# Two transformer blocks on one core: the shared expert's products spread over group two, the last scatter halved, one weight split moved

## The reference, cut to what matters

```python
def hier_moe(h, ...):
    t = h.reshape(-1, d)
    # each token: the best group, then the best 2 of its 8 experts, with weights "combine"
    a = jnp.einsum('nd,edf->nef', t, w_gate)
    b = jnp.einsum('nd,edf->nef', t, w_up)
    hid = jax.nn.silu(a) * b * combine[:, :, None]
    routed = jnp.einsum('nef,efd->nd', hid, w_down)
    shared = (jax.nn.silu(t @ w_sh_gate) * (t @ w_sh_up)) @ w_sh_down
    return (routed + shared).reshape(bsz, slen, d)

# first_block, at its end
h = h + rms_norm(ffn, post_ffn_norm[l])
# second_block, at its start
u = rms_norm_2(h, norm_mix[l])
proj = u @ w_in[l]
z_pool, q, k, v, g_pool, g_attn = jnp.split(proj, splits, axis=-1)
```

## Time and profile before

| what | us |
| --- | --- |
| median of 3 runs | 738.94 (738.7 to 742.1) |
| the profiled execution | 737.79 |
| its span in the profile | 736.0 |
| TensorE busy in the span | 667.2 (91%) |
| VectorE, ScalarE, POOL busy | 331.8, 280.9, 46.9 |
| weight stream | 182.23 MB in all, mean 248 GB/s over the span |

### The profile page before, as it was taken

The page is one execution under the profiler, slowest core; times in us unless marked ns, Lnnn a source line. Parts: engine busy times, 40 slices in busy tenths (PEclk is TensorE's granted clock), DMA queues, the critical chain, the costliest instruction groups (busy, mean ns, idle before and its releaser), DMA issues.

```text
span 736.0 us, 10953 instructions
## 1 busy us (share of the span) xinstructions
PE 667.2 (91%) x4473; PEld 517.5 (70%) x4473; DVE 331.8 (45%) x607; ACT 280.9 (38%) x529; POOL 46.9 (6%) x68
## 2 busy tenths in 40 slices
PE   8999899898677895778889999999989999999996
PEld 5979787734212741133359999989789999999994
DVE  8676555631101011011056566647755544445554
ACT  7655563312001010011055666573555433344432
POOL 1000102000001000000037200000000000000000
PEclk9999999999777999688999999999999999999998
DMA  9926309599999959999995444335525455455201
GB/s 355 419 92 228 115 8 420 231 364 415 423 420 421 403 217 422 423 420 420 423 420 205 172 145 143 115 123 197 196 104 183 172 183 211 179 174 192 93 1 58
DMA packets 26145, 182.23 MB, mean 248 GB/s; under 512 B 3040, under 2 KB 3168, under 8 KB 4464
## 3 DMA queue, kind: packets, MB, share of 16 engines
q1 hardware_dynamic: 25344, 178.81, 62.1%
q10 hardware_dynamic: 752, 2.73, 0.9%
HBM read 180.48 MB, written 1.05 MB: 247 GB/s over the span
## 4 chain that ended last, share of the span: by engine, by line
PE 66%; DMA 19%; DVE 7%; ACT 4%; issue 2%; POOL 1%; SPq 0%; DVEq 0%; POOLq 0%; ACTq 0%
PE ps L1377 64%; DMA ring<-stream_dram 18%; PE ps L1380 2%; DVE ring_r L362 2%; ACT single L355 1%; DMA vec<-small_dram 1%; DVE work L1331 1%; ACT work L768 1%; DVE work L1334 0%; DVE turned L1290 0%; POOL stat L810 0%; DVE turned L1350 0%; POOL stat L872 0%; ACT work L696 0%; ACT turned L773 0%
## 5 line engine op out<-in xcount | busy, mean ns | idle before, releaser
L1377 PE MATMUL ps<-turned,single 128*128 128x256 f32 (+1 forms) x1312 | 240.1, 285 | 2.9 <-DVE turned L1350 1.2
L1377 PEld LDWEIGHTS ps<-turned,single 128*128 128x128 f32 x1312 | 203.0, 189 | 6.0 <-issue 2.9
L1377 PE MATMUL ps<-turned,ring_r 128*128 128x256 f32 (+1 forms) x656 | 185.5, 283 | 0.0
L362 DVE TENSOR_TENSOR ring_r<-ring,single 128x1024 fp32r<-128x1024 f32 x134 | 160.8, 1243 | 49.4 <-ACT single L355 49.4
L1377 PE MATMUL ps<-ring,work 128*32 128x512 f32 (+2 forms) x814 | 134.1, 666 | 32.9 <-DMA ring<-stream_dram 28.5
L355 ACT ACTIVATE single<-ring 128x1024 fp32r<-128x1024 f32 x134 | 133.8, 1049 | 2.2 <-DMA ring<-stream_dram 1.7
L1377 PEld LDWEIGHTS ps<-turned,ring_r 128*128 128x128 f32 x656 | 124.0, 189 | 0.0
L1377 PEld LDWEIGHTS ps<-ring,work 128*32 128x32 f32 (+1 forms) x814 | 38.1, 127 | 107.9 <-DMA ring<-stream_dram 62.5
L1377 PE MATMUL ps<-single 128*128 128x512 f32 (+1 forms) x299 | 64.6, 363 | 3.6 <-DVE single L1244 2.0
L1377 PEld LDWEIGHTS ps<-single 128*128 128x128 f32 x299 | 47.0, 197 | 28.8 <-issue 15.6
L1377 PE MATMUL ps<-single,turned 128*128 128x512 f32 (+3 forms) x208 | 59.8, 365 | 3.1 <-DVE turned L1054 1.8
(11 more groups left out here) (227 smaller groups left out, 576.3 us busy)
## 6 DMA issues: line engine op xcount, KB each, us to landing
ring<-stream_dram SPq DMA_DIRECT2D x161, 1024.0 KB, 11.8
work<-stream_dram SPq DMA_DIRECT2D x5, 1024.0 KB, 13.0
turned_w<-stream_dram SPq DMA_DIRECT2D x2, 1024.0 KB, 13.6
gain<-gains_dram ACTq DMA_DIRECT2D x3, 512.0 KB, 8.2
cst<-consts_dram ACTq DMA_DIRECT2D x1, 1066.0 KB, 9.0
h<-x_dram SPq DMA_DIRECT2D x2, 512.0 KB, 4.1
out_dram<-work SPq DMA_DIRECT2D x4, 256.0 KB, 2.0
vec<-small_dram SPq DMA_DIRECT2D x1, 451.5 KB, 5.8
```

The source lines that it names most:

```text
L362: dve.tensor_tensor(ring_r[:, place, a], ring[:, place, a], w_hi[k % HIGHS][:, a].bitcast(F32), ALU.subtract).then_inc(s["wlo_done"], 1)
L1377: return pe.matmul(o, lhsT, rhs, start=start, stop=stop, **kw)
```

## The change

It has three parts.

1. The shared gate entry comes behind the third gate/up entry of group 1's second half, the up entry behind the sixth, the shared down entry behind the group's last. The products of each stand at the same places on TensorE, in banks 6 and 7; SiLU and the hidden product stand ahead of the half's own; TensorE waits for them ahead of `down`. The turning (now into bank 4) and the shared down products stay between groups 1 and 2. POOL's four memsets wait for an earlier count of `used`.
2. In the last half of the last group, `scatter(p, 0)` stands between the third and the fourth down entry, in place of the 4 idle products there. The squares and the gain products of column half 0 stand ahead of the copy and the split of column half 1. `used` for the last entry is counted by the other half of the scatter.
3. VectorE splits the first half of entry `SPLIT1` behind the last low part of u, ahead of the second. TensorE does all products with that entry's high weights first (two chunks), then those with its low weights.

```diff
-SHARED_GROUP = 2
-SHARED_AT = MOE_AT + SHARED_GROUP * MOE_GROUP
+SHARED_GROUP = 1
+SHARED_BEHIND = {2: 0, 5: 1}
+SH_GATE_AT = MOE_AT + SHARED_GROUP * MOE_GROUP + Q_SLOTS + 3
+SH_UP_AT = SH_GATE_AT + 4
+SH_DOWN_AT = MOE_AT + (SHARED_GROUP + 1) * MOE_GROUP + 2
...
+            def sum_squares(n):
+                for i in range(NT):
+                    act.wait_ge(s["moe_done"], 1 + n * (i + 1))
+                    act.activation(xn2[:, i, column_half(n)], ps[:, 2 * i + n, :], ACT.Square, accum_out=(ssc, ssc2)[n][:, i:i + 1]
+                                   ).then_inc(s["ss_done"], 1)
...
                 for p in range(PAIRS):
+                    if shared and p == PAIRS - 1:
+                        shared_silu()
                     act.wait_ge(s["gu_ps"], it * PAIRS + (p + 1))
...
                     for n in range(2):
+                        if ending and p == PAIRS - 1 and n:
+                            sum_squares(0)
                         act.wait_ge(s["y_ps"], it * (2 * PAIRS) + (2 * p + n + 1))
...
-            pool.wait_ge(used, SHARED_AT)
+            pool.wait_ge(used, ASIDE_END)
...
+            def with_moe_gain(i, n):
+
+                dve.wait_ge(s["ss_done"], 6 + 2 * n + i)
+                a = column_half(n)
+                dve.tensor_tensor(mixb[:, i, a], ps[:, 2 * i + n, :], gain[:, a], ALU.mult).then_inc(s["gmoe_done"], 1)
...
                 for p in range(PAIRS):
+                    if shared and p == PAIRS - 1:
+                        shared_hidden()
                     dve.wait_ge(s["sg_done"], it * PAIRS + (p + 1))
...
                     for n in range(2):
+                        if ending and p == PAIRS - 1 and n:
+                            with_moe_gain(0, 0)
+                            with_moe_gain(1, 0)
                         dve.wait_ge(s["yh_done"], it * (2 * PAIRS) + (2 * p + n + 1))
...
-            for i, n in ((0, 0), (0, 1), (1, 0), (1, 1)):
-
-                dve.wait_ge(s["ss_done"], (6, 8, 7, 9)[2 * i + n])
...
+            with_moe_gain(0, 1)
+            with_moe_gain(1, 1)
             for i in range(NT):
                 dve.wait_ge(s["rs_done"], 5 + i + 1)
-                dve.wait_ge(s["gmoe_done"], 2 * i + 2)
+                dve.wait_ge(s["gmoe_done"], 3 + i)
...
-            split_low_half(dve, SPLIT1, 0)
             dve.wait_ge(s["rs_done"], 7 + 1)
...
-            split_low_half(dve, SPLIT1, 1)
-            for n in range(1, 8):
+            for n in range(0, 8):
                 split_low(dve, SPLIT1 + n)
...
+            def shared_gate_up(b):
+
+                n = (SH_GATE_AT, SH_UP_AT)[b]
+                slot_ready(pe, n)
+                for i in range(NT):
+                    for t in range(DT):
+                        last = mm(ps[:, 6 + i, b * FF:(b + 1) * FF], tT[:, t, i * P:(i + 1) * P],
+                                  home(n)[:, t * FF:(t + 1) * FF], t == 0, t == DT - 1)
+                        if i == t == 0:
+                            last.then_inc(used, 1)
+                    if b:
+                        last.then_inc(s["sgu_ps"], 1)
...
                         if t == 1 and p:
                             scatter(p - 1, 1)
+                        if shared and p and t in SHARED_BEHIND:
+                            shared_gate_up(SHARED_BEHIND[t])
...
                     for n in range(2):
                         for j in range(FF // P):
-                            keep_warm(p)
+                            if not (n and j):
+                                keep_warm(p)
...
+                            if split_scatter(p) and n and j == 0:
+                                scatter(p, 0)
...
-                            if n == i == k == 0:
+                            if i == k == 0 and n == int(split_scatter(p)):
                                 end.then_inc(freed, 1)
...
+                    if shared and p:
+                        pe.wait_ge(s["hs_done"], NT)
                     down(p)
-                    scatter(p, 0)
+                    if not split_scatter(p):
+                        scatter(p, 0)
...
-            for c in range(4):
-                chunk(ps[:, c, 0:TOK], SPLIT1 + c // 2, c % 2, (u_hi, u_lo), frees=1 if c == 2 else 0,
-                      turned_from=11 if c == 0 else None).then_inc(s["z2_ps"], 1)
+            for c in range(2):
+
+                pe.wait_ge(s["whi_done"], 2 * SPLIT1 + c + 1)
+                for t in range(DT):
+                    if c == 0:
+                        pe.wait_ge(s["turn_dve"], 11 + t + 1)
+                    w = w_hi[SPLIT1 % HIGHS][:, c * D + t * P:c * D + (t + 1) * P]
+                    mm(ps[:, c, 0:TOK], w, u_hi[:, t, :], t == 0, False, skip_group_check=True)
+                    mm(ps[:, c, 0:TOK], w, u_lo[:, t, :], False, False, skip_group_check=True)
+            for c in range(2):
+                split_ready(SPLIT1, c)
+                for t in range(DT):
+                    last = mm(ps[:, c, 0:TOK], split_pair(SPLIT1)[1][:, c * D + t * P:c * D + (t + 1) * P], u_hi[:, t, :],
+                              False, t == DT - 1, skip_group_check=True)
+                last.then_inc(s["z2_ps"], 1)
+            for c in range(2, 4):
+                chunk(ps[:, c, 0:TOK], SPLIT1 + 1, c % 2, (u_hi, u_lo), frees=1 if c == 2 else 0).then_inc(s["z2_ps"], 1)
```

More of the change, by code:

```diff
@@ L373, in entry_at @@
         def entry_at(n):
-            if n < MOE_AT or n >= SHARED_AT + 3:
+            if n < MOE_AT or n > SH_DOWN_AT:
                 return n
-            return n + 3 if n < SHARED_AT else SH_GATE + n - SHARED_AT
+            shared = {SH_GATE_AT: SH_GATE, SH_UP_AT: SH_UP, SH_DOWN_AT: SH_DOWN}
+            return shared[n] if n in shared else n + 3 - sum(at < n for at in shared)
         def place2(n):
@@ L658, in shared_silu, with column_half, moe_group @@
                     act.wait_ge(s["sgu_ps"], i + 1)
-                    act.activation(sg_s[:, i, :], ps[:, 4 + i, 0:FF], ACT.Silu, scale=rsb[:, i:i + 1]
+                    act.activation(sg_s[:, i, :], ps[:, 6 + i, 0:FF], ACT.Silu, scale=rsb[:, i:i + 1]
                                    ).then_inc(s["ssg_done"], 1)
-            def moe_group(it):
+            def column_half(n):
+                return slice(n * 512, (n + 1) * 512)
+            def sum_squares(n):
[3 more added lines that the diff above has]
+                                   ).then_inc(s["ss_done"], 1)
+            def moe_group(it, shared=False, ending=False):
                 for t in (0, 1, 4, 5):
@@ L678, in _ @@
             for g in range(LOOPED):
[L679 to L681 removed]
+                moe_group(g, g == SHARED_GROUP)
             act.wait_ge(s["rounds_done"], 1)
@@ L686, in _ @@
                 moe_group(it)
-            moe_group(final)
-            def column_half(n):
-                return slice(n * 512, (n + 1) * 512)
-            for n, sums in enumerate((ssc, ssc2)):
-                for i in range(NT):
-                    act.wait_ge(s["moe_done"], 1 + n * (i + 1))
-                    act.activation(xn2[:, i, column_half(n)], ps[:, 2 * i + n, :], ACT.Square, accum_out=sums[:, i:i + 1]
-                                   ).then_inc(s["ss_done"], 1)
+            moe_group(final, ending=True)
+            sum_squares(1)
             split_high_half(act, SPLIT1, 0)
@@ L1213, in shared_hidden, with shared_rows, column_half, moe_group @@
                     dve.wait_ge(s["ssg_done"], i + 1)
-                    dve.scalar_tensor_tensor(hs_tok[:, i, :], ps[:, 4 + i, FF:2 * FF], rsb[:, i:i + 1], sg_s[:, i, :],
+                    dve.scalar_tensor_tensor(hs_tok[:, i, :], ps[:, 6 + i, FF:2 * FF], rsb[:, i:i + 1], sg_s[:, i, :],
                                              ALU.mult, ALU.mult).then_inc(s["hs_done"], 1)
+            def shared_rows():
                 dve.wait_ge(s["hst_ps"], 1)
-                dve.tensor_copy(hs, halves(ps[:, 6, :], TOK)).then_inc(s["hst_sb"], 1)
-            def moe_group(it, ranks=None, ahead=None, first=False):
+                dve.tensor_copy(hs, halves(ps[:, 4, :], TOK)).then_inc(s["hst_sb"], 1)
+            def column_half(n):
+                return slice(n * 512, (n + 1) * 512)
+            def with_moe_gain(i, n):
+                dve.wait_ge(s["ss_done"], 6 + 2 * n + i)
+                a = column_half(n)
+                dve.tensor_tensor(mixb[:, i, a], ps[:, 2 * i + n, :], gain[:, a], ALU.mult).then_inc(s["gmoe_done"], 1)
+            def moe_group(it, ranks=None, ahead=None, first=False, shared=False, ending=False):
                 for t in (2, 6):
@@ L1674, in shared_down, with moe_group @@
                             last = mm(ps[:, 2 * i + n, :], hs[:, f, i * P:(i + 1) * P],
-                                      home(SHARED_AT + 2)[:, f * D + n * 512:f * D + (n + 1) * 512], False, False,
+                                      home(SH_DOWN_AT)[:, f * D + n * 512:f * D + (n + 1) * 512], False, False,
                                       skip_group_check=True)
```

(11 more changed lines are left out.)

39 lines of the change are left out of this document (8 added, 31 removed).

## The result

Measured beside each other on one chip, the kernel before took 739.71 us and the changed one **727.87 us** (five runs: 727.15, 727.61, 727.87, 728.52, 731.42). The ratio is 0.9837, 95% interval 0.9808 to 0.9866: about 12 us less. Forecast: 728.7 us, range 726.5 to 733.0. The changed kernel's profiled execution is the slowest of its five, 731.42 us with a span of 729.6, so its rows carry disturbances that the median does not.

What follows compares the result with a forecast made beforehand. The mixture stage was taken to be bound by its stream of 1 MB weight entries, with a 9.05 us hole between groups. 738.94 - 9.05 - 1.15 = 728.7 us; range 726.5 to 733.0.

Steps and rivals of the forecast that it cites:

- Bound and hole: Mixture stage: paced by 1 MB weight entries every 2.483 us; the stream's hole between two groups closes, -9.05 us.
- Replay of the shared blocks: Group one's second half: TensorE at full clock does the spread shared products and reaches group two's first entry at 256.4.
- What I gave 0.14: Rival: clock low for one shared block, leaving part or all of the hole, 731.1 to 738 us; chance 0.14.
- Slack of 2.5 us: Weight stream at group two's start: least slack of a freed slot ahead of its turn is 2.5 us.
- A clock fall of the size that I put at 731.1: Shared gate at half clock: group two starts at 261.3, a hole of 2.4 us stays; within a rival of chance 0.14.
- Part 2's last scatter: Mixture's tail: last scatter 0.5 us later through queued squares and gain products, won back behind; residual 0.15 us sooner.
- The sign that I named: Mixture's tail: the last scatter would come half a microsecond later behind the last down entry.
- Part 3: Ahead of block 2: without VectorE's split, POOL's 1.71 us tensor_scalar ends 1.2 us earlier.
- Block 2's order: Block 2's first chunks: high products first hide the later weight split, 0 us, bounds -0.3 to +0.5.
- Sum of the tail: Last scatter split and later weight split together: -1.15 us, bounds +0.5 to -1.7.
- The path that I named as next: Behind the last scatter: 26 idle products, 8 turns and 4 idle ones let the last turns come at most 1.63 us sooner.
- Sum: Whole kernel: -9.05 - 1.15 = -10.2 us, from 738.94 to 728.7 us.

Runs made afterwards that it cites:

- part 1 alone: Only the shared products spread over group one, on the kernel before: 728.56 us, ratio 0.9851.
- the second profile: The changed kernel, no edit, profiled once more: 730.03 us, span 728.2; median of that set 728.09 us, ratio 0.984.
- the first profile: The changed kernel's profiled execution in the main measurement, slowest of its five runs: 731.42 us, span 729.6.
- these doses: Changed kernel with 20 or 40 idle products of 512 columns between shared down and group two's gather: 733.97 us (0.9912) and 736.91 us (0.9964).
- all, first half of the split back: Changed kernel with the first half of the weight split back between residual and norm, high products still first: 729.20 us, 0.9863.
- the experiment with the old one: Changed kernel with block 2's first two chunks in the old order, high and low products for each piece: 733.86 us, 0.9903.
- part 2 alone: Only the last scatter split, with its squares and gain products, on the kernel before: 739.91 us, 0.999.
- part 3 alone: Only the weight split moved behind the last low part of u, high products first, on the kernel before: 740.40 us, 0.9987.
- all, three entries without idle products: Changed kernel without the 4 idle products ahead of each of the last half's first three gate/up entries: 727.23 us (0.9828), again 726.46 us (0.9813).
- the smaller dose: Changed kernel with 20 idle products of 512 columns between shared down and group two's gather: 733.97 us, 0.9912.

## Why the prediction was right

- **Bound and hole** (-9.05): right. The last gate/up entry is 9.15 us sooner with part 1 alone and 9.33 in the second profile, and with one late entry of each run taken out the hole is 9.1 (above); group two starts at 256.11 and 256.56 (forecast 256.4). In the first profile it is 7.92, of which 0.9 is that the entries were late already ahead of the change's place. The digit 8 in slice 9 also lies ahead of it.
- **Replay of the shared blocks**: right. They ran at full clock in one block of 18.98 us; the clock from 214 to 266 is 1.00 in both profiles of the changed kernel. What I gave 0.14 did not happen. The Trainium skill, "TensorE: Matmul & The Clock Gate", section "HAM oscillation — how this bites in real kernels", advises to bunch work that DMA waits cut up; the trace agrees in the direction that matters here, since bunched blocks replaced entries of 1.07 us of work in 2.48 and the 0.61 became 1.00.
- **Slack of 2.5 us**: mis-sized. 0.5 to 0.9 us are free. Two terms failed. SyncE's issue was taken at 257.3, 0.9 behind a product of 256.4, and found 2.08 behind it; and the refill of a dry queue, put at one period per entry, lost 1.4 and 0.95 more. It did no harm, as TensorE was on time: here the forecast was helped by the clock staying up. A clock fall of the size that I put at 731.1 would by these doses have cost about 2 us more than that (an estimate).
- **Part 2's last scatter** (+0.5): mis-sized, +0.15. I let the gain products start at 372.5 and 373.25 one by one. They ran back to back, 1.29 us in all, and the split followed 2.03 behind the start of the last down products, not 2.37. The residual is then 0.46 sooner, not 0.15. The sign that I named, the last scatter half a microsecond later, was not seen.
- **Part 3** (POOL's slow instruction 1.2 sooner): right. Residual to last turns 5.98 instead of 7.11 us, so -1.13, and by taking the split back alone the 7.11 return. The Trainium skill, "SBUF — State Buffer", section "Who interferes with whom", says that only VectorE and GpSimd contend, for a shared pair of ports that one instruction holds until it ends. By it POOL's small one waits for VectorE's split to end; the trace agrees: it ended 0.12 to 0.14 us behind it in four kernels, and where the split is gone it takes 0.57 us. Its record begins at 379.84 in the kernel before, while VectorE's residual still runs and ahead of the split (380.20); without the split it ends 0.13 behind the residual (373.62 and 373.49). So it waits for VectorE in both cases, for two instructions in the one and one in the other.
- **Block 2's order** (0): right. Last turns to the end of block 2's chain of products: 36.60 us before, 36.66 after. This order makes part 3 free; the experiment with the old one showed the price, 5.2 us.
- **Sum of the tail** (-1.15): -1.5, inside its bound of -1.7. The path that I named as next, scatter and 26 idle products, is now the one that bounds: the turns start without a wait at its end. The scatter starts 0.35 sooner than I had it (0.15 later than before and not 0.5), and that is the difference. Whether fewer idle products there would bring the turns forward was not tried. The best measure is one distance, from the last gate/up entry to the group of 30 products that opens attention:

| kernel | from, to | distance | against before |
|---|---|---|---|
| before | 361.13, 422.00 | 60.87 | |
| part 1 alone | 351.98, 412.87 | 60.89 | +0.02 |
| part 2 alone | 361.29, 421.72 | 60.43 | -0.44 |
| part 3 alone | 365.13, 424.95 | 59.82 | -1.05 |
| all, first half of the split back | 352.01, 412.51 | 60.50 | -0.37 |
| all, three entries without idle products | 351.40, 410.75 | 59.35 | -1.52 |

The changed kernel itself has 60.93 and 60.94 in its two profiles; 1.6 of each is the clock's fall at 356 us, which leaves 59.3. The parts add up: -0.44 - 1.05 = -1.49.
- **Sum**: -9.15 - 1.5 = -10.7 us by the measured terms, forecast -10.2. Measured is 1.63% of 740, -12.1, with an interval of 9.9 to 14.2, which holds both. The rest may be the kernel before, whose medians beside these kernels (739.7 to 741.0) lie above its profiled execution (737.79); what it loses in its slower runs was not looked at. One way is in the profile of part 3 alone: with the hole still there, a fall of the clock in the shared down products made it 1.7 us longer, while the changed kernel kept 1.00 there in both profiles. How often that happens is not known. So of the 12 us only these 10.7 have a shown cause.

## What to carry to other kernels

Where a stage is paced by a ring of transfers, count what the other work frees: work that frees few slots belongs between the entries, where the queue of landed ones covers it, and not between two groups. Idle products meant to keep the clock up must leave the engine time to catch up: compare the period that they make (2.12 us here) with the stream's (2.48). What they cost here is small, 0.6 and 0.7 us in the two profiles whose last gate/up entry no longer waits for the stream. When a low-precision remainder is moved later, put the products that don't need it ahead of the wait, or the wait holds all of them.

## Unexpected of the hardware

- The clock fell in some profiles and not in others at the same place of code that is the same there: at about 356 us, behind gaps of 0.99 and 0.47 us, in three of the thirteen profiles besides the kernel before's (one of them the smaller dose's, at 361 us), and at attention's first products, behind a stand of 0.75 us after 35 us without a longer one, in three. Each fall cost 1.5 to 1.6 us. What decides it was not found.
- An issue from SyncE's dynamic loop came 2.08 us behind the start of the products whose first entry it waited for, 1.2 behind TensorE's count, four times alike.
- A queue that had run dry cost 1.4 and 0.95 us beyond the lateness of the first issue, lost within the three entries that follow it.
